# Hybrid encoder block on one core: hidden blocks 19 and 20 by seven products, and 22 sums of w_down quarters made by DRAM transfers

## The chip, the core and the metric

The kernel runs on one core of a Trainium2 chip. The metric is the device time in microseconds of one execution. Matmuls run on PE (TensorE), elementwise work on DVE (VectorE) and ACT (ScalarE); POOL (GpSimd) does a few small operations and issues some DMAs; SP issues nearly all others. All operands are float32, and every product is made of three matmuls of float32r parts: with a = a_hi + a_lo and w = w_hi + w_lo it is w_hi a_hi + w_hi a_lo + w_lo a_hi. ACT makes the high parts by a cast, DVE the low parts by a subtraction.

## The reference

```python
# SEQ = 512, D_MODEL = 1024, FFN_HIDDEN = 2816 (22 blocks of 128), DEPTH = 1
for l in range(DEPTH):
    h = rms_norm(x, attn_norm[l])
    proj = h @ w_in[l]      # q, k, v, forget logits, pool input, conv x/B/C, gates
    y_a = forgetting_attention(...) @ w_proj_attn[l]      # 8 heads x 64
    y_b = multiscale_pool(u, pool_w[l], pool_scale[l]) @ w_proj_pool[l]
    y_c = short_gated_conv(cv, cb, cc, conv_w[l]) @ w_proj_conv[l]
    mixed = gates[..., 0, :] * y_a + gates[..., 1, :] * y_b + gates[..., 2, :] * y_c
    x = x + mixed @ w_out[l]
    h = rms_norm(x, ffn_norm[l])
    a, b = jnp.split(h @ w_gate_up[l], 2, axis=-1)
    x = x + (jax.nn.silu(a) * b) @ w_down[l]
return rms_norm(x, final_norm)
```

## The kernel before, in words

Each engine runs a program written out by hand; semaphores tie them together, and no scheduler moves anything. The stages, in the order of the table STAGES, are: norm; front; pair (four attention passes of two heads each); mix and rounds (branch gates and projections); out (the product with w_out); ffn_first, ffn_head, turns and ffn_last (the 22 hidden blocks); down (the product with w_down).

A hidden block needs 128 gate columns and 128 up columns of w_gate_up over 1024 rows. A plain block (`gate_up`) does it in 2 units of 8 products of a 128 x 128 weight tile and 512 tokens. A turn (v counts them) does it by Winograd's scheme on quarters: 4 rows of weight tiles by gate or up, 256 tokens by half, seven products F11, F21, F2, F1, F3, F22, F4 of 4 tiles each. The sums of activations it needs (sums_hi, sums_lo) are made once; the sums of weight quarters are made in each turn by DVE (`turn_sums`, `turn_last_sum`), which also adds the partial products up (`turn_post`) and makes the hidden rows (`turn_hidden`). Blocks 0 to 3 are plain, 4 to 18 are the 15 turns, 19 to 21 are plain in ffn_last.

Two hidden blocks make a tile of down. `hid_sum(r)` makes tile r's four sums, `hidden_hi` and `hid_low` their parts. The product with w_down is by Winograd too, over R = 11 tiles: the first phase takes A11 with the quarter (2r, 1) and S1 with the sum of both quarters of block 2r, the later ones take sums with more quarters and the rest. Before the change DVE makes all sums of w_down: `first_sum` (11), two in each `second_sums` (22) and `third_sum` (11). `chain(r)` is the place of the running sum; for r of 3 and more it lies in the area that holds the operand of the plain blocks and turns.

Weights come by SP's queue into three slots of `raw` (load 6 of down into a spare place), their parts go to three slots of whi and wlo, in down to a ring of nine half slots. x2, the residual, is kept in DRAM (x2_kept) during the turns and comes back in ffn_last, one of four loads behind each unit from the third on.

POOL issues for each attention pass four small transfers of two rows of forget sums (L880, L882), those of passes 1 to 3 when the score products of the pass before are done (full6). Behind those of the last pass it waits for norm_var, which comes in ffn_first. PE waits for them (f_in) ahead of the score products.

Of the kernel before, what the change touches and what calls it, by code (L numbers as in the profile page):

```python
# [26 lines left out]
P = 128  # L27
# [9 lines left out]
          ("ffn_first", 1, 2), ("ffn_head", 1, 6), ("turns", 1, 105),  # L37
          ("ffn_last", 1, 6), ("down", 1, 77)]
# [7 lines left out]
TURNS = range(4, 19)  # L46
# [9 lines left out]
    "free2": dict(front=1, pair=1, mix=1, out=4, ffn_head=1, ffn_last=1),  # L56
    "free3": dict(front=1, pair=5, mix=1, out=4, ffn_head=1, ffn_last=1),
    "free4": dict(front=2, pair=4, mix=2, out=2, ffn_head=1, ffn_last=1),
    "free5": dict(front=3, pair=4, mix=1, out=2, ffn_head=1, ffn_last=1),
# [20 lines left out]
    "vector_step": dict(norm=11, front=23, pair=5, mix=6, rounds=8, ffn_first=3, ffn_head=5, turns=7, ffn_last=4,  # L80
# [30 lines left out]
def loads_before(stage, i, j):  # L111

    first, per = stage_of(stage)
    if stage in LATER + LAST_STAGES:
        first -= PARTS - LOADS
    if stage in LAST_STAGES:
        first -= PER_TURN * len(TURNS) - TURN_LOADS
    return (first + j + i * per) // SLOTS + 1


def hybrid_block(nc, x, attn_norm, w_in, b_forget, b_gate, w_proj_attn, pool_w, pool_scale,
# [26 lines left out]
    with ExitStack() as ctx:  # L148
# [36 lines left out]
        w_sums = nc.dram_tensor("w_sums", [16 * P, D // 2], F32, kind="Internal").ap()  # L185
        x2_kept = nc.dram_tensor("x2_kept", [S, D], F32, kind="Internal").ap()
# [189 lines left out]
        SUMMED = list(TILES.values()) + [0, 1, 9, 10]  # L376
# [116 lines left out]

        def down_raw(k, half, n=1):
# [62 lines left out]
        out_summed, sums_kept = sem("out_summed"), sem("sums_kept")  # L557
        mix_summed, mix_hi, mix_lo = sem("mix_summed"), sem("mix_hi"), sem("mix_lo")
# [32 lines left out]
        def _(sp):  # L591
            def load(stage, i, j, halves, width=P):
# [7 lines left out]
                elif stage == "ffn_last" and j < SLOTS:  # L600
                    v, part, sums = ((-2, F22, 3), (-1, F21, 4), (-1, F22, 4))[j]
                    v += len(TURNS)
                    sp.wait_ge(w_lo, turn_part(v, part) + 1)
                    sp.wait_ge(turn_summed, 4 * v + sums)
# [6 lines left out]
                for src, at in halves:  # L611
# [4 lines left out]
                                 ).then_inc(landed[s], 16)  # L616

# [152 lines left out]
            for j in range(3):  # L770
                for n, c in enumerate(gate_up_columns(19 + j)):
# [2360 lines left out]
```

## Time and profile before

| | |
|---|---|
| median of 3 runs | 770.66 us (770.55 to 770.76) |
| the profiled execution's own time | 770.3 us |
| its span, first to last instruction | 768.5 us |
| PE busy | 759.5 us (99%) |
| DVE, ACT, POOL busy | 649.4, 420.7, 18.3 us |
| moved by DMA | 99.46 MB, mean 129 GB/s |

The span is the part that the trace covers; 1.8 us of the execution lie around it. Matmuls are pipelined and their durations overlap, so what one costs is read from start to start. An idle time of an engine counts only where PE ends up waiting for it.

### The profile page before, as it was taken

How to read it: one execution, taken by the hardware profiler on the slowest of the kernel's cores; microseconds unless marked ns; L12 is line 12 of the kernel's file. 1: busy time of each engine (PE TensorE's matmuls, PEld its weight loads, DVE VectorE, ACT ScalarE, POOL GpSimd, SP SyncE). 2: the span in 40 equal slices, each digit the busy share in tenths (PEclk: the TensorE clock that was granted, in tenths of full speed). 3: DMA queues.
4: the chain of work that ended last, by engine and by line, in shares of the span. 5: the costliest groups of instructions: out<-in, count | busy, mean ns of one | idle time of the engine just before them, and what ended most of it. 6: DMA issues, size and time to landing. Idle time of an engine off the chain costs nothing.

```text
span 768.5 us, 12215 instructions
## 1 busy us (share of the span) xinstructions
PE 759.5 (99%) x4451; PEld 675.3 (88%) x4451; DVE 649.4 (85%) x1041; ACT 420.7 (55%) x712; POOL 18.3 (2%) x41
## 2 busy tenths in 40 slices
PE   8999999999999999999999999999999999999997
PEld 7888888888889999999988888999999998888885
DVE  7788976767798969777787899899999985899997
ACT  6536556646544646555455745555555552655554
POOL 2001100100000000000000000000000000000001
PEclk9999999999999999999999999999999999999999
DMA  8963542324133443344376533333333364443423
GB/s 301 306 202 82 166 111 56 84 55 110 46 93 83 111 127 93 83 110 113 107 269 197 192 111 94 103 106 110 110 101 98 106 209 147 141 161 133 149 89 110
DMA packets 133311, 99.46 MB, mean 129 GB/s; under 512 B 5932, under 2 KB 114532, under 8 KB 133252
## 3 DMA queue, kind: packets, MB, share of 16 engines
q1 hardware_dynamic: 132596, 98.35, 42.4%
q8 instruction: 36, 0.59, 0.3%
q10 hardware_dynamic: 144, 0.26, 0.1%
q14 instruction: 23, 0.19, 0.1%
q0 software_dynamic: 512, 0.07, 0.1%
HBM read 90.21 MB, written 8.39 MB: 128 GB/s over the span
## 4 chain that ended last, share of the span: by engine, by line
PE 98%; DMA 0%; issue 0%; ACT 0%; DVE 0%; POOL 0%; POOLq 0%; DVEq 0%
PE bank L917 10%; PE bank L913 10%; PE bank L915 10%; PE bank L1350 7%; PE bank L1348 7%; PE bank L1346 7%; PE bank L1161 4%; PE bank L1400 4%; PE bank L1159 4%; PE bank L1401 4%; PE bank L1402 4%; PE bank L1157 4%; PE bank L1195 2%; PE bank L1196 2%; PE bank L1197 2%; PE bank L1258 2%
## 5 line engine op out<-in xcount | busy, mean ns | idle before, releaser
L913 PE MATMUL bank<-operands,whi 128*128 128x512 f32 x352 | 137.9, 392 | 0.0
L917 PE MATMUL bank<-operands,wlo 128*128 128x512 f32 x352 | 137.1, 390 | 0.0
L915 PE MATMUL bank<-operands,whi 128*128 128x512 f32 x352 | 137.0, 389 | 0.0
L2078 DVE TENSOR_TENSOR wlo<-raw,whi 128x1024 fp32r<-128x1024 f32 x61 | 74.2, 1223 | 16.8 <-ACT whi L1466 16.0
L1466 ACT CAST whi<-raw 128x1024 fp32r<-128x1024 f32 x61 | 64.1, 1050 | 26.4 <-PE bank L917 7.6
L917 PEld LDWEIGHTS bank<-operands,wlo 128*128 128x128 f32 x352 | 66.1, 188 | 13.9
L915 PEld LDWEIGHTS bank<-operands,whi 128*128 128x128 f32 x352 | 66.1, 188 | 13.3
L913 PEld LDWEIGHTS bank<-operands,whi 128*128 128x128 f32 x352 | 66.1, 188 | 13.3
L1346 PE MATMUL bank<-sums_hi,whi 128*128 128x256 f32 x240 | 67.9, 283 | 0.0
L1348 PE MATMUL bank<-sums_lo,whi 128*128 128x256 f32 x240 | 67.9, 283 | 0.0
L1350 PE MATMUL bank<-sums_hi,wlo 128*128 128x256 f32 x240 | 67.9, 283 | 0.0
L1348 PE MATMUL bank<-operands,whi 128*128 128x256 f32 x180 | 50.9, 283 | 0.0
L1350 PE MATMUL bank<-operands,wlo 128*128 128x256 f32 x180 | 50.9, 283 | 0.0
L1346 PE MATMUL bank<-operands,whi 128*128 128x256 f32 x180 | 50.9, 283 | 0.0
L1346 PEld LDWEIGHTS bank<-sums_hi,whi 128*128 128x128 f32 x240 | 46.1, 192 | 0.0
L1348 PEld LDWEIGHTS bank<-sums_lo,whi 128*128 128x128 f32 x240 | 46.1, 192 | 0.0
L1350 PEld LDWEIGHTS bank<-sums_hi,wlo 128*128 128x128 f32 x240 | 46.1, 192 | 0.0
L1161 PE MATMUL bank<-sums_hi,wlo 128*128 128x256 f32 x160 | 45.3, 283 | 0.0
L1159 PE MATMUL bank<-sums_lo,whi 128*128 128x256 f32 x160 | 45.3, 283 | 0.0
L1157 PE MATMUL bank<-sums_hi,whi 128*128 128x256 f32 x160 | 45.2, 283 | 0.0
L2421 DVE TENSOR_TENSOR wlo<-raw,whi 128x1024 fp32r<-128x1024 f32 (+1 forms) x40 | 38.1, 952 | 3.2 <-ACT whi L1652 3.2
L2823 DVE TENSOR_TENSOR wlo<-raw,whi 128x1024 fp32r<-128x1024 f32 x30 | 36.6, 1220 | 4.1 <-ACT whi L1893 4.1
(323 smaller groups left out, 1995.9 us busy)
## 6 DMA issues: line engine op xcount, KB each, us to landing
raw<-in_w_in_dram SPq DMA_DIRECT2D x105, 256.0 KB, 3.3
raw<-in_w_gate_up_dram SPq DMA_DIRECT2D x88, 256.0 KB, 3.3
raw<-in_w_down_dram SPq DMA_DIRECT2D x53, 256.0 KB, 3.0
big_x<-in_x_dram SPq DMA_DIRECT2D x8, 512.0 KB, 5.3
tiles<-in_w_out_dram SPq DMA_DIRECT2D x4, 1024.0 KB, 7.2
w_sums<-tiles SPq DMA_DIRECT2D x4, 1024.0 KB, 7.2
raw<-w_sums SPq DMA_DIRECT2D x16, 256.0 KB, 3.1
raw<-in_w_out_dram SPq DMA_DIRECT2D x12, 256.0 KB, 3.5
```

Source lines behind the costliest of these rows:

```text
L913: nc.tensor.matmul(banks[b][:, 0:width], whi[:, s, w], op(hi + k * S), start=a, stop=False)
L915: nc.tensor.matmul(banks[b][:, 0:width], whi[:, s, w], op(lo + k * S), start=False, stop=False)
L917: mm = nc.tensor.matmul(banks[b][:, 0:width], wlo[:, s, w], op(hi + k * S), start=False, stop=z)
L1157: nc.tensor.matmul(to, wh[:, w], xh, start=first and k == 0, stop=False, skip_group_check=not first)
L1159: nc.tensor.matmul(to, wh[:, w], xl, start=False, stop=False, skip_group_check=not first)
L1161: mm = nc.tensor.matmul(to, wl[:, w], xh, start=False, stop=k == 3, skip_group_check=not first)
L1346: nc.tensor.matmul(to, wh[:, w], xh, start=first and k == 0, stop=False, skip_group_check=not first)
L1348: nc.tensor.matmul(to, wh[:, w], xl, start=False, stop=False, skip_group_check=not first)
L1350: mm = nc.tensor.matmul(to, wl[:, w], xh, start=False, stop=k == 3, skip_group_check=not first)
L1466: nc.scalar.copy(whi[:, s, :], raw[:, s, :]).then_inc(w_hi, 1)
L2078: nc.vector.tensor_tensor(wlo[:, s, :], raw[:, s, :], whi[:, s, :].bitcast(F32), ALU.subtract).then_inc(w_lo, 1)
L2421: nc.vector.tensor_tensor(part_at(wlo, r, j, n), src, part_at(whi, r, j, n).bitcast(F32), ALU.subtract).then_inc(w_lo, n)
```

## The change

Two things at once:

- TURNS grows from blocks 4..18 to 4..20, so blocks 19 and 20 go by seven products and ffn_last keeps block 21 alone, in banks 0 and 1. Since its two units fall into other slots, its loads take the raw slot of `last_slot(j)`, and the places of down's ring are moved by a slot. In the last turn DVE makes the hidden sums of tiles 0 and 1.
- 22 of the sums of w_down quarters are made in DRAM, in a new tensor down_sums of 2 x 1408 rows of 512: `copy_down(kind)` copies a quarter of each of the 11 block pairs, `add_down(kind)` adds a second by an accumulating DMA. POOL issues the first copy behind its transfers for the third attention pass, and the first add, the second copy and the second add behind those for the fourth. SP waits for both adds (down_added) before w_down's loads; in the first two phases of down one of a load's two transfers is now such a sum, in the first phase straight to `chain(r)`. `first_sum` is gone, and `second_sums` has one addition for two. Down's loads 3 and up now stand behind the wait for the end of block 21 on PE (used >= NU), where before only load 6 and up did. x2's four loads move to behind down's loads 6 to 9.

```diff
-          ("ffn_first", 1, 2), ("ffn_head", 1, 6), ("turns", 1, 105),
-          ("ffn_last", 1, 6), ("down", 1, 77)]
+          ("ffn_first", 1, 2), ("ffn_head", 1, 6), ("turns", 1, 119),
+          ("ffn_last", 1, 2), ("down", 1, 77)]
...
-TURNS = range(4, 19)
+TURNS = range(4, 21)
...
+def last_slot(j):
+
+    return (stage_of("turns")[0] - PARTS + LOADS + TURN_LOADS + j) % SLOTS
...
+        down_sums = nc.dram_tensor("down_sums", [2 * FH // 2, D // 2], F32, kind="Internal").ap()
...
+            at = (at + NU % SLOTS * 2 * S) % (2 * SLOTS * S)
...
@@ SP
-            for j in range(3):
-                for n, c in enumerate(gate_up_columns(19 + j)):
-                    load("ffn_last", 0, 2 * j + n, c)
-                    t = 2 * j + n - 2
-                    if t == 0:
-                        sp.wait_ge(used, turn_part(len(TURNS) - 1, F22) + 1)
-                    if t >= 0:
-                        sp.dma_start(big_x[:, t * D:(t + 1) * D], x2_kept[t * P:(t + 1) * P, :]
-                                     ).then_inc(x2_back, 16)
+            for n, c in enumerate(gate_up_columns(TURNS[-1] + 1)):
+                load("ffn_last", 0, n, c)
...
+            sp.wait_ge(down_added, 32)
             for r in range(R):
-                if r == SPARE:
+                if r == SLOTS:
                     sp.wait_ge(used, NU)
-                elif r == SPARE + SLOTS:
+                if r == 0:
+                    sp.wait_ge(used, turn_part(LAST_TURN, F22) + 1)
+                if r == SPARE + SLOTS:
                     sp.wait_ge(w_lo, NU + 2 * (SPARE - SLOTS) + 2)
-                else:
+                elif r < SLOTS - LAST_UNITS:
+                    turn_raw_read(LAST_UNITS + r)
+                elif r != SPARE:
                     sp.wait_ge(w_lo, NU - SLOTS + r + 1 if r < SLOTS else NU + 2 * (r - SLOTS) + 2)
                 sp.sem_inc(loads_begun, 1)
-                load_down(r, [(2 * r, 1), (2 * r, 0)])
+                load_down(r, [(down_block(2 * r, 1), down_raw(r, 0)),
+                              (down_sum(0)[r * P:(r + 1) * P, :], chain(r))])
+                if SPARE <= r < SPARE + TB:
+                    t = r - SPARE
+                    sp.dma_start(big_x[:, t * D:(t + 1) * D], x2_kept[t * P:(t + 1) * P, :]
+                                 ).then_inc(x2_back, 16)
...
-                load_down(R + r, [(2 * r, 0), (2 * r + 1, 0)])
+                load_down(R + r, [(down_sum(1)[r * P:(r + 1) * P, :], down_raw(R + r, 0)),
+                                  (down_block(2 * r + 1, 0), down_raw(R + r, 1))])
...
@@ POOL
+            down = w_down.rearrange("(r e p) c -> p r e c", e=2, p=P)
+            def summed_rows(kind):
+                return down_sum(kind).rearrange("(r p) c -> p r c", p=P)
+            def copy_down(kind):
+                c = 1 - kind
+                pool.dma_start(summed_rows(kind), down[:, :, 0, c * HALF:(c + 1) * HALF]
+                               ).then_inc(down_copied, 16)
+            def add_down(kind):
+                pool.wait_ge(down_copied, 16 * (kind + 1))
+                pool.dma_start(summed_rows(kind), down[:, :, kind, 0:HALF], accum_op=ALU.add
+                               ).then_inc(down_added, 16)
...
                     pool.dma_start(op(K2[a], S, slice(at, at + 2)).bitcast(F32), f_pair
                                    ).then_inc(f_in, 16)
+                if i == 2:
+                    copy_down(0)
+                elif i == 3:
+                    add_down(0)
+                    copy_down(1)
+                    add_down(1)
...
@@ PE
+            pe.wait_ge(turn_gates, 2 * LAST_TURN)
+            pe.wait_ge(turn_posted, 4 * LAST_TURN)
             gate_up("ffn_last", 0, 0)
             pe.wait_ge(turn_gates, 2 * len(TURNS))
             pe.wait_ge(turn_posted, 4 * len(TURNS))
-            for j in range(1, 3):
-                gate_up("ffn_last", 0, j)
...
@@ DVE
-            def first_sum(r):
-                dve.wait_ge(*landed_down(r))
-                if r == 3:
-                    dve.wait_ge(used, NU)
-                nc.vector.tensor_tensor(chain(r), down_raw(r, 0), down_raw(r, 1),
-                                        ALU.add).then_inc(summed, 1)
...
-                b12, b22 = raw[:, s, 0:HALF], raw[:, s, HALF:2 * HALF]
-                nc.vector.tensor_tensor(b12, b12, b22, ALU.add).then_inc(summed, 1)
+                b22 = raw[:, s, HALF:2 * HALF]
                 nc.vector.tensor_tensor(chain(r), chain(r), b22, ALU.add).then_inc(summed, 1)
```

The order on DVE at the end of the last turn before the change, and into the first plain block (bank6, bank5: partial products of the turn; wlo<-raw: low parts of a plain unit; tiles: hidden sums):

```order
L2831 TENSOR_TENSOR work<-bank6,work 128x256
L2078 TENSOR_TENSOR wlo<-raw,whi 128x1024
L2831 TENSOR_TENSOR work<-bank5,work 128x256
L2723 TENSOR_TENSOR operands<-tiles_32_50,operands 128x512
L2839 SCALAR_TENSOR_TENSOR tiles_32_50<-work 128x512
L2078 TENSOR_TENSOR wlo<-raw,whi 128x1024
L2709 TENSOR_TENSOR tiles_32_50<-tiles_32_50 128x512
```

The same place after the change, down to the first part of w_down (L2712):

```order
L2867 TENSOR_TENSOR work<-bank6,work 128x256
L2121 TENSOR_TENSOR wlo<-raw,whi 128x1024
L2745 TENSOR_TENSOR tiles_32_50<-tiles_32_50 128x512
L2750 SCALAR_TENSOR_TENSOR tiles_32_50<-tiles_32_50 128x256
L2753 SCALAR_TENSOR_TENSOR tiles_32_50<-tiles_32_50 128x256
L2745 TENSOR_TENSOR tiles_32_50<-tiles_32_50 128x512
L2750 SCALAR_TENSOR_TENSOR tiles_32_50<-tiles_32_50 128x256
L2753 SCALAR_TENSOR_TENSOR tiles_32_50<-tiles_32_50 128x256
L2867 TENSOR_TENSOR work<-bank5,work 128x256
L2759 TENSOR_TENSOR operands<-tiles_32_50,operands 128x512
L2875 SCALAR_TENSOR_TENSOR last_tile_32_52<-work 128x512
```

The hidden sums of tiles 0 and 1 stood behind the turn's last addition (work<-bank5) and a third unit's split, and now stand ahead of that addition.

On POOL, the end of its transfers of forget rows before the change:

```order
L880 DMA operands<-big_y 2x512
L882 DMA operands<-big_y 2x512
L880 DMA operands<-big_y 2x512
L882 DMA operands<-big_y 2x512
L887 TENSOR_TENSOR stat<-stat 128x4
```

And after it, from the last transfer for the third pass on:

```order
L925 DMA operands<-big_y 2x512
L906 DMA down_sums<-in_w_down_dram 128x11x512
L923 DMA operands<-big_y 2x512
L925 DMA operands<-big_y 2x512
L923 DMA operands<-big_y 2x512
L925 DMA operands<-big_y 2x512
L912 DMA down_sums<-in_w_down_dram 128x11x512
L906 DMA down_sums<-in_w_down_dram 128x11x512
L912 DMA down_sums<-in_w_down_dram 128x11x512
L936 TENSOR_TENSOR stat<-stat 128x4
```

The fourth pass's forget rows now stand behind the first copy, the rest of the DRAM transfers behind them.

On SP, from the last gate and up columns on, before the change:

```order
L777 DMA big_x<-x_kept 128x1024
L615 DMA raw<-in_w_gate_up_dram 128x4x128 x2
L777 DMA big_x<-x_kept 128x1024
L785 DMA raw<-in_w_down_dram 128x512 x12
L785 DMA early_49<-in_w_down_dram 128x512 x2
```

And after it, from load 5 of down on:

```order
L800 DMA raw<-in_w_down_dram 128x512
L800 DMA early_49<-down_sums 128x512
L800 DMA early_49<-in_w_down_dram 128x512
L800 DMA early_49<-down_sums 128x512
L819 DMA big_x<-x_kept 128x1024
L800 DMA raw<-in_w_down_dram 128x512
L800 DMA early_49<-down_sums 128x512
L819 DMA big_x<-x_kept 128x1024
```

x2's loads (big_x<-x_kept) stood among the plain blocks' loads and now stand among those of down.

## Rows read from the trace of the kernel before

**Rows 1.** The page, first part: span, and PE's busy time.

```profile
span 768.5 us, 12215 instructions
...
PE 759.5 (99%) x4451; PEld 675.3 (88%) x4451; DVE 649.4 (85%) x1041; ACT 420.7 (55%) x712; POOL 18.3 (2%) x41
```

**Rows 2.** The page, fourth part: the chain that ended last.

```profile
PE 98%; DMA 0%; issue 0%; ACT 0%; DVE 0%; POOL 0%; POOLq 0%; DVEq 0%
```

**Rows 3.** Windows (turns; plain blocks; down): PE, PEld, DVE, ACT, POOL busy, PEclk, DMA share, GB/s.

```profile
474.04:625.23 151.19, 151.19 (x1261) 151.19 (x1260) 139.89 (x220) 84.06 (x141) 0.00 (x0) 1.00 0.37 106
...
625.23:657.90 32.67, 32.67 (x147) 27.03 (x145) 21.00 (x31) 11.35 (x17) 0.00 (x0) 1.00 0.56 182
657.90:687.00 29.10, 29.10 (x130) 24.11 (x129) 28.00 (x43) 19.60 (x29) 0.00 (x0) 1.00 0.52 174
```

**Rows 4.** Timeline of PE at the borders (start us, us, engine, line, operation).

```profile
474.04 0.28 PE L1346 MATMUL bank<-operands,whi 128*128 128x256 f32 x1
...
625.23 0.40 PE L913 MATMUL bank<-operands,whi 128*128 128x512 f32 x1
```

**Rows 5.** Timeline of DVE, last turn and plain block 19.

```profile
625.12 1.23 DVE L2078 TENSOR_TENSOR wlo<-raw,whi 128x1024 fp32r<-128x1024 f32 x1 [1.32 <-ACT whi L1466]
628.94 0.69 DVE L2709 TENSOR_TENSOR tiles<-tiles 128x512 f32<-128x512 f32 x1
...
630.46 0.68 DVE L2709 TENSOR_TENSOR tiles<-tiles 128x512 f32<-128x512 f32 x1
```

**Rows 6.** Timeline of ACT, then of DVE, start of down.

```profile
661.30 1.28 ACT L1979 ACT_TABLE_LOAD   x1
...
662.60 0.68 DVE L2676 TENSOR_TENSOR early<-raw 128x512 f32<-128x512 f32 x1
663.24 0.69 DVE L2668 TENSOR_TENSOR operands<-raw,operands 128x512 fp32r<-128x512 f32 x1
...
664.45 0.69 DVE L2668 TENSOR_TENSOR operands<-early,operands 128x512 fp32r<-128x512 f32 x1
```

**Rows 7.** Timeline of POOL's DMA issues, third pass's last, fourth pass's first and last.

```profile
116.38 0.57 POOL L882 DMA_DIRECT2D operands<-big_y  x1
149.48 0.54 POOL L880 DMA_DIRECT2D operands<-big_y  x1 [32.52 <-PE bank L1089]
...
151.08 0.58 POOL L882 DMA_DIRECT2D operands<-big_y  x1
```

**Rows 8.** The page, third part (packets, MB, share) and sixth (KB, us to landing).

```profile
q0 software_dynamic: 512, 0.07, 0.1%
...
raw<-in_w_in_dram SPq DMA_DIRECT2D x105, 256.0 KB, 3.3
...
raw<-in_w_down_dram SPq DMA_DIRECT2D x53, 256.0 KB, 3.0
...
w_sums<-tiles SPq DMA_DIRECT2D x4, 1024.0 KB, 7.2
...
operands<-big_y POOLq DMA_DIRECT2D x16, 4.0 KB, 1.6
```

**Rows 9.** Windows of two stretches dense with transfers.

```profile
85.00:97.00 12.00, 12.00 (x69) 10.23 (x68) 10.88 (x20) 5.96 (x15) 0.00 (x0) 1.00 0.84 264
384.00:397.00 13.00, 13.00 (x66) 11.05 (x65) 9.67 (x15) 7.07 (x9) 0.00 (x0) 1.00 0.82 292
```

**Rows 10.** Timelines of SP, PE, ACT and DVE, fourth attention pass.

```profile
174.14 1.01 SPq L615 DMA_DIRECT2D raw<-in_w_in_dram  x2
...
180.39 0.28 PE L1087 MATMUL bank<-operands 128*128 128x256 f32 x1
...
186.23 1.06 ACT L1466 CAST whi<-raw 128x1024 fp32r<-128x1024 f32 x1
...
189.72 1.27 DVE L2307 TENSOR_SCALAR big_y<-big_y,stat 128x128 f32<-128x128 f32 x4
...
195.08 0.49 PE L1102 MATMUL bank<-ident,big_y 128*128 128x128 f32 x3
```

More of the change, by code:

```diff
@@ L55 @@
     "free1": dict(front=1, pair=2, mix=1, out=3, ffn_first=1, ffn_head=1, ffn_last=1),
[L56 to L59, printed above, removed]
+    "free2": dict(front=1, pair=1, mix=1, out=4, ffn_head=1),
+    "free3": dict(front=1, pair=5, mix=1, out=4, ffn_head=1),
+    "free4": dict(front=2, pair=4, mix=2, out=2, ffn_head=1),
+    "free5": dict(front=3, pair=4, mix=1, out=2, ffn_head=1),
     "free6": dict(front=2, pair=4, mix=1, out=2, ffn_first=1),
@@ L78 @@
     "v_lo_part": dict(pair=2),
-    "vector_step": dict(norm=11, front=23, pair=5, mix=6, rounds=8, ffn_first=3, ffn_head=5, turns=7, ffn_last=4,
+    "vector_step": dict(norm=11, front=23, pair=5, mix=6, rounds=8, ffn_first=3, ffn_head=5, turns=10, ffn_last=1,
                         down=3),
@@ L599, in load @@
                     sp.sem_inc(loads_begun, 1)
[L600 to L604, printed above, removed]
+                elif stage == "ffn_last":
+                    s = last_slot(j)
+                    turn_raw_read(j)
                     sp.sem_inc(loads_begun, 1)
@@ L616, in load, with turn_raw_read @@
                                  ).then_inc(landed[s], 16)
+            def turn_raw_read(m):
+                v, part, sums = ((-2, F22, 3), (-1, F21, 4), (-1, F22, 3))[m]
+                v += len(TURNS)
+                sp.wait_ge(w_lo, turn_part(v, part) + 1)
+                sp.wait_ge(turn_summed, 4 * v + sums)
             def columns(w, col):
@@ L781, in load_down, with down_block @@
-            def load_down(k, blocks):
+            for n, c in enumerate(gate_up_columns(TURNS[-1] + 1)):
+                load("ffn_last", 0, n, c)
+            def down_block(row, c):
+                return w_down[row * P:(row + 1) * P, c * HALF:(c + 1) * HALF]
+            def load_down(k, parts):
                 signal = spare_in if k == SPARE else landed[k % SLOTS]
-                for at, (row, c) in enumerate(blocks):
-                    sp.dma_start(down_raw(k, at),
-                                 w_down[row * P:(row + 1) * P, c * HALF:(c + 1) * HALF]
-                                 ).then_inc(signal, 16)
+                for src, to in parts:
+                    sp.dma_start(to, src).then_inc(signal, 16)
@@ L1311, in gate_up @@
             def gate_up(stage, i, j):
-                a = (2 * j + 2) % 6
+                a = (2 * j + 2) % 6 if stage == "ffn_head" else 0
                 k = j // 3 + 1
@@ L2009, in _ @@
             for rows in ROWS4:
-                act.wait_ge(summed, 3 * R + rows[-1] + 1)
+                act.wait_ge(summed, R + rows[-1] + 1)
                 for at, n in in_one(U_4 + rows[0], len(rows)):
@@ L2872, in _ @@
                 turn_post(v, 3, 3, 2, u, 1)
-                if last:
+                if not last:
+                    turn_lo(v + 1, F2, turn_sum(0, 2), 2)
+                else:
                     split_lo("ffn_last", 0, 1)
-                else:
-                    turn_lo(v + 1, F2, turn_sum(0, 2), 2)
+                    hid_sum(0)
+                    wait_free(dve, 1, "ffn_head", 0, 1)
+                    hid_sum(1)
                 dve.wait_ge(used, turn_part(v, F22) + 1)
```

78 lines of the change are left out of this document (32 added, 46 removed).

## The prediction

> **What bounds the kernel now.** The first view is the page: the engines' busy shares and the chain that ended last. PE, the matmul engine, is busy for 759.5 of 768.5 us [rows 1], and 98% of the chain is PE following PE [rows 2]. So time leaves only with matmuls that leave, and comes only with a wait that makes PE stand. The second view is the windows around the two stages that change [rows 3]: from 474.04 to 657.90 PE is busy for every us, DVE for 139.89 of 151.19 us in the turns and for 21.00 of 32.67 in the three plain blocks behind them. The third is PE's timeline at the borders [rows 4], by which the windows are cut; the durations there (0.28, 0.40) overlap, so what a matmul costs is its window divided by the count.
>
> **PE's work.** The 15 turns (seven products) run from 474.04 to 625.23: 151.19/15 = 10.08 us each. The three plain blocks run from 625.23 to 657.90: 32.67/3 = 10.89 us each [rows 3, 4]. A turn is 7 x 4 x 3 = 84 matmuls of 256 columns, a plain block 2 x 8 x 3 = 48 of 512, so columns fall by an eighth, but the narrow ones cost more per column: 10.08/84 = 0.120 us against 10.89/48 = 0.227, and 10.08 is 0.926 of 10.89. Blocks 19 and 20 become turns: 2 x (10.89 - 10.08) = 1.62 us less. Nothing else on PE changes in number: down keeps its products. Turns would end at 474.04 + 17 x 10.08 = 645.4, block 21 at 656.3, where down begins, for 657.9 before. Matmuls run at the same clock on both sides of the border (granted 1.00 in both windows, the 2.4 GHz level), so the pitches carry over.
>
> **The last turn and block 21.** I move the rows of the last turn [rows 5] by 2 x 10.08 = 20.16 us. DVE's second split for block 21 starts at 645.3 and takes 1.2 us. Behind it stand the hidden sums of tiles 0 and 1, ahead of the turn's last addition from its bank: 1.5 us each (628.94 to 630.46), so they end near 649.5. The turn's last addition, tile 9's low part, the turn's product, two more low parts and the first two w_down parts follow: seven of at most 0.6 us (the pitch of 512 columns in [rows 6]), to 653.7. PE wants all of it at 656.3: 2.6 us left. This backlog had three plain blocks to drain in and now has one; that is the cover which thins.
>
> **Start of down.** Load 3 and those behind it now wait on SP for PE to finish block 21, because a sum lands straight in the operand area; before, only the DVE sum waited. Issued at 656.5 and 656.9, at 3.0 us each [rows 8], they land near 660. ACT meanwhile does load 2's parts (two casts, 1.1), the last tile's high part behind scaled and hid_sum on DVE (659.8) and the table load (1.3 us [rows 6]), so it takes load 3 at 661.1, and DVE ends its low parts at 662.9. PE asks at 656.3 + 3 steps of 12 matmuls at 32.67/144 = 0.227 us, 664.4: 1.5 us left. Before, the same parts ended at 665.1 [rows 6] for a PE that asked at 657.9 + 8.2 = 666.1, so 1.0 was left. I charge nothing.
>
> **What leaves DVE.** Of the 44 quarter sums of w_down on DVE 22 go: 22 x 0.6 us of pitch (662.60 to 663.24 [rows 6]) = 13 us of DVE in down. That hurries only what PE already finds ready: between 657.90 and 687.00 PE is busy for 29.10 of 29.10 us with DVE at 28.00 [rows 3]. I credit nothing.
>
> **x2 comes back later.** Its four loads of 512 KB move from the plain blocks (182 GB/s in that window, rows 3) into down's loads 6 to 9. From 656.5 to load 10 there are 8 x 0.524 + 4 x 0.524 = 6.3 MB. Load 10 must be in 1.9 us ahead of PE (656.3 + 10 x 2.72 = 683.5), and data flows some 1.8 us behind the first issue: 23.3 us, or 270 GB/s. The two dense stretches of the trace moved 264 at a share of 0.84 and 292 at 0.82 [rows 9], so full engines give 314 to 356. It fits, by 3 us at 314.
>
> **The transfers.** One moves 11 x 128 rows of 2 KB, 2.88 MB. POOL issues the first copy behind the third pass's rows (116.9), and add, copy, add behind the fourth's (151.7) [rows 7]. The trace has no DRAM-to-DRAM and no adding transfer. For a copy the low end is 2.88 MB / 356 GB/s = 8 us, the high end the store of w_sums, 7.2 us for 1.05 MB [rows 8], so 20 us. An add also reads its target, twice a copy: 16 to 40. The three behind 151.7 take 40 to 100 us and end between 192 and 252. I take 16 for an add, since w_sums' row is a landing time with loads queued beside it, and so an end near 195. SP wants them near 644: never late.
>
> What they can cost is the loads beside them. The tightest of the fourth pass is issued at 174.14 and lands near 178 (issue 0.4 us apart, 3.3 [rows 8]); ACT takes it at 186.23, ahead of the second head's exponentials, and their probabilities end at 191.0 for a PE that asks at 195.08 [rows 10]. Allowance: 8.2 + 4.1 = 12.3 us. A pair of loads is 64 packets of 512 bytes an engine. If engines took one 2 KB packet of the transfers for each, at 2 KB / (314/16 GB/s) = 104 ns it would be 6.7 us later, at twice that for an add 13.3; fair halves by bytes, 1.7. Two of the three fit. I charge nothing. The Trainium skill's "DMA: Bandwidth & Descriptors", section "Queues, rings and completion order", says that an engine changes queues at packets that hold some 9 to 17 descriptors; by that a pair of loads would be interrupted 4 to 7 times, not 64, and the sum would stay at nothing. No row here shows it.
>
> POOL has to write the rows' descriptors itself, and the fourth pass's F rows stand behind the first copy. PE asks for them at 180.39 [rows 10]; they take 2.2 us to issue and 1.6 to land. So the copy may hold POOL until 176.6: 59.7 us, 42 ns a row. Below, it costs nothing. The nearest rows are those F issues, two rows in 0.54 us [rows 7], where the fixed part is not told apart: 270 ns a row if all of it were per row, near nothing if none. By packets it is 17 ns, for the 16 issues made 512 packets [rows 8], 32 each; I take that, 24 us for 1408 rows. The Trainium skill, "SBUF — State Buffer", "Who interferes with whom", speaks against the change here: descriptors that GpSimd writes wait while VectorE holds the port pair that the two share. The F issues, beside a DVE at work, all took 0.54 to 0.58, so the trace shows no such wait; by the rule POOL would take longer, and the sum would change only past 42 ns a row.
>
> **Sum.** Profiled: span 768.5 - 1.62 = 766.9, and 770.3 with the 1.8 around it becomes 768.7. The median of the runs, 770.66, lies 0.36 above the profiled run, so 769.0. That is 0.21% down, and 0.2% (1.54 us, to 769.12) is about what a measurement tells from no change: the forecast sits on that line.
>
> **Rivals.**
> 1. The transfers hold up the loads (slower). For: the allowance ends at 12.3/64 = 192 ns a packet, and twice 104 is over it; in the rounds from 232.8 on, a transfer still running would meet loads that are taken as they land. Against: fair sharing costs 1.7, and only 88 packets an engine exist per transfer. Price: 1.0 us at 208 ns, and at the high end (7.2 us per 32 packets = 225, doubled 450) 64 x 0.45 - 12.3 = 16.5. I take 5: 774.0. It decides from some 240 ns on.
> 2. Down starts late. For: 1.5 us at load 3, 2.6 at load 0, and x2 on the same queue. Price: at 250 GB/s 6.3 MB take 25.2 us, 1.9 late: 770.9, within 0.2%. Against: measured rates.
> 3. POOL is held past 176.6. At 270 ns a row the copy holds it 380 us, to 497; PE would stand from 180.4 to some 501: 320 us, 1089.
> 4. The saving isn't all there (a turn at the end pays a wait on DVE's backlog, where DVE is 93% busy): 0.8 of 1.62, 769.8.
>
> **Chances.** Forecast 0.66, rival 1 0.14, rival 2 0.11, rival 3 0.03, rival 4 0.06. The forecast's own range is 768.8 to 769.3 (0.1 of the runs' spread, 0.2 of small gaps); some 0.7 of it lies under 769.12. Faster: 0.66 x 0.7 and a little that DVE's relief might give: 0.48. Slower: 0.14 + 0.03 = 0.17. Within: 0.35. Range: down to 768.7; up to 771.1, which takes in rivals 2 and 4 and leaves out most of 1 and 3.
>
> **What would show it.** Right: PE's windows again without a gap, 17 turns at 10.08 us, down beginning 1.6 us earlier, POOL's copy issue under 60 us, the adding transfers landed before 232.8, landing times of w_in loads from 117 to 200 under 12 us. Wrong: idle time on PE at the score products (L1087) or probability transposes (L1102) of passes three and four, or on the first products of down behind w_down parts; or POOL issue rows of tens of us.

## The result and the profile after

The changed kernel takes 774.54 us (median of 4 runs, 772.36 to 775.52), the kernel before 770.71 in the same comparison: the ratio is 1.0046, with a 95% interval from 1.0025 to 1.0067. It is slower, and above the range of the forecast (768.7 to 771.1). The profiled execution took 772.36 us.

The first and third part of the page and its list of DMA issues answer to [rows 1, 8]: PE is busy for as long as before in a span 2.0 us longer, although it has fewer columns to do.

```profile
span 770.5 us, 12395 instructions
...
PE 759.6 (99%) x4523; PEld 677.9 (88%) x4523; DVE 648.2 (84%) x1039; ACT 426.1 (55%) x724; POOL 24.5 (3%) x45
...
q0 software_dynamic: 4800, 11.60, 6.4%
...
down_sums<-in_w_down_dram POOLq DMA_DIRECT2D x4, 2816.0 KB, 21.2
```

The windows over turns, block 21 and down, cut as in [rows 3], show the saving that was forecast: 171.35/17 = 10.08 us a turn, 10.91 for block 21, and no idle time on PE. The turns began at 477.71 and not at 474.04, so 3.67 us were lost ahead of them. Of these 0.37 were there before the first transfer (a load that the kernel before issues at 112.03 is issued at 112.40); the fourth attention pass makes the other 3.3.

```profile
477.71:649.06 171.35, 171.35 (x1430) 171.35 (x1428) 158.88 (x250) 95.31 (x160) 0.00 (x0) 1.00 0.36 103
649.06:659.97 10.91, 10.91 (x51) 9.02 (x49) 10.77 (x18) 5.76 (x10) 0.00 (x0) 1.00 0.41 142
659.97:690.00 30.03, 30.03 (x134) 24.89 (x133) 24.04 (x37) 19.68 (x30) 0.00 (x0) 1.00 0.82 280
...
659.97:764.92 104.95, 104.95 (x469) 86.97 (x467) 90.96 (x128) 61.25 (x94) 2.14 (x3) 1.00 0.46 159
```

The chain of waits around the only long gap (start, us, what; the fourth attention pass) says where. The second half of a weight load, issued at 166.05, lands 16.49 us later; ACT casts it, DVE makes its low parts, and only then does DVE take the first head's row maxima (L2335), which free the banks for the second head's score products (L1136). Before, the same load landed 3.5 us behind its issue at 165.66, at 169.1, and ACT took it at 179.02.

```profile
166.05 16.49 DMA raw<-in_w_in_dram
182.54 0.02 issue
182.56 1.05 ACT whi L1516
...
183.64 1.23 DVE wlo L2121
...
184.90 0.29 DVE big_y L2335
...
185.25 0.38 PE bank L1136
```

The window around it in the kernel before has 24 matmuls and no idle time; the changed kernel's, shown under the run again, has 9 and 2.3 us without any. The rest of the 3.3 us is matmuls that start far apart behind the gap.

```profile
182.50:187.00 4.50, 4.50 (x24) 3.72 (x23) 3.78 (x17) 3.54 (x10) 0.00 (x0) 1.00 0.40 116
```

The timeline of ACT and DVE in the kernel before shows the same three steps without a wait: parts at 180.10, row maxima at 181.36.

```profile
179.02 1.05 ACT L1466 CAST whi<-raw 128x1024 fp32r<-128x1024 f32 x1
180.10 1.23 DVE L2078 TENSOR_TENSOR wlo<-raw,whi 128x1024 fp32r<-128x1024 f32 x1 [0.97 <-ACT whi L1466]
181.36 0.29 DVE L2291 CUSTOM_DVE_ANT_0 big_y<-bank,flat 128x128 f32<-128x128 f32 x1
```

POOL's timeline of its issues (start, us) answers to [rows 7]: one copy in the third pass, add and copy back to back in the fourth, and the second add once the copy has landed.

```profile
117.33 1.14 POOL L906 DMA_DIRECT2D down_sums<-in_w_down_dram  x1
...
152.04 2.04 POOL L912 DMA_DIRECT2D down_sums<-in_w_down_dram  x1
153.20 1.96 POOL L906 DMA_DIRECT2D down_sums<-in_w_down_dram  x1
182.46 1.87 POOL L912 DMA_DIRECT2D down_sums<-in_w_down_dram  x1 [27.30 <-DMA down_sums<-in_w_down_dram]
```

How a load comes to 16 us is in the DMA queues of two stretches, 160 to 171 us beside the first add and 174 to 180 beside the second copy (packets, MB, share of 16 engines; q0 carries the transfers, q1 the loads).

```profile
q0 software_dynamic: 910, 1.86, 91.0%
q1 hardware_dynamic: 908, 0.46, 21.0%
```

```profile
q0 software_dynamic: 492, 2.01, 86.8%
q1 hardware_dynamic: 504, 0.25, 14.7%
```

The two queues moved as many packets as each other. One of an add took 0.910 x 16 x 11 us / 910 = 176 ns and one of a copy 169, one of a load 41 and 28. The 64 packets an engine of a load are thus stretched to 64 x 217 ns = 13.9 us beside an add. The load issued at 154.7 needed until 172.4; the one issued at 165.6 stood behind it in SP's queue and then met the second copy.

### The profile page after: what moved, and what is told of

It reads as the page before. It is cut to its first block, busy times and chain, and to the rows that moved or that the text cites. A ratio compares the mean times of both kernels' runs of the same rounds, so it can differ in the third digit from the quotient of the medians.

```text
span 770.5 us, 12395 instructions
## 1 busy us (share of the span) xinstructions
PE 759.6 (99%) x4523; PEld 677.9 (88%) x4523; DVE 648.2 (84%) x1039; ACT 426.1 (55%) x724; POOL 24.5 (3%) x45
## 4 chain that ended last, share of the span: by engine, by line
PE 95%; DMA 3%; DVE 1%; issue 1%; ACT 1%; POOL 0%; POOLq 0%; SPq 0%; DVEq 0%
PE bank L962 9%; PE bank L966 9%; PE bank L964 9%; PE bank L1399 7%; PE bank L1397 7%; PE bank L1395 7%; PE bank L1451 4%; PE bank L1210 4%; PE bank L1208 4%; PE bank L1449 4%; PE bank L1206 4%; PE bank L1450 4%; PE bank L1244 2%; PE bank L1245 2%; PE bank L1246 2%; DMA raw<-in_w_in_dram 2%
## 5 line engine op out<-in xcount | busy, mean ns | idle before, releaser
L962 PE MATMUL bank<-operands,whi 128*128 128x512 f32 x320 | 125.4, 392 | 0.0
L966 PE MATMUL bank<-operands,wlo 128*128 128x512 f32 x320 | 124.7, 390 | 0.0
L964 PE MATMUL bank<-operands,whi 128*128 128x512 f32 x320 | 124.6, 389 | 0.0
L1397 PE MATMUL bank<-sums_lo,whi 128*128 128x256 f32 x272 | 77.0, 283 | 0.0
L1395 PE MATMUL bank<-sums_hi,whi 128*128 128x256 f32 x272 | 77.0, 283 | 0.0
L1399 PE MATMUL bank<-sums_hi,wlo 128*128 128x256 f32 x272 | 77.0, 283 | 0.0
L1516 ACT CAST whi<-raw 128x1024 fp32r<-128x1024 f32 x57 | 59.9, 1050 | 29.8 <-PE bank L966 7.6
L964 PEld LDWEIGHTS bank<-operands,whi 128*128 128x128 f32 x320 | 60.1, 188 | 12.1
L962 PEld LDWEIGHTS bank<-operands,whi 128*128 128x128 f32 x320 | 60.1, 188 | 12.1
L1397 PE MATMUL bank<-operands,whi 128*128 128x256 f32 x204 | 57.7, 283 | 0.0
L1399 PE MATMUL bank<-operands,wlo 128*128 128x256 f32 x204 | 57.7, 283 | 0.0
L1395 PE MATMUL bank<-operands,whi 128*128 128x256 f32 x204 | 57.7, 283 | 0.0
L1397 PEld LDWEIGHTS bank<-sums_lo,whi 128*128 128x128 f32 x272 | 52.2, 192 | 0.0
L1210 PE MATMUL bank<-sums_hi,wlo 128*128 128x256 f32 x160 | 45.3, 283 | 0.0
L1208 PE MATMUL bank<-sums_lo,whi 128*128 128x256 f32 x160 | 45.3, 283 | 0.0
L1206 PE MATMUL bank<-sums_hi,whi 128*128 128x256 f32 x160 | 45.2, 283 | 0.0
L1944 ACT CAST whi<-raw 128x1024 fp32r<-128x1024 f32 x34 | 35.6, 1046 | 11.5 <-PE bank L1399 9.3
## 6 DMA issues: line engine op xcount, KB each, us to landing
down_sums<-in_w_down_dram POOLq DMA_DIRECT2D x4, 2816.0 KB, 21.2
```

The lines of the kernel that those rows point to most:

```text
L962: nc.tensor.matmul(banks[b][:, 0:width], whi[:, s, w], op(hi + k * S), start=a, stop=False)
L964: nc.tensor.matmul(banks[b][:, 0:width], whi[:, s, w], op(lo + k * S), start=False, stop=False)
L966: mm = nc.tensor.matmul(banks[b][:, 0:width], wlo[:, s, w], op(hi + k * S), start=False, stop=z)
L1206: nc.tensor.matmul(to, wh[:, w], xh, start=first and k == 0, stop=False, skip_group_check=not first)
L1208: nc.tensor.matmul(to, wh[:, w], xl, start=False, stop=False, skip_group_check=not first)
L1210: mm = nc.tensor.matmul(to, wl[:, w], xh, start=False, stop=k == 3, skip_group_check=not first)
```

## The experiments

Twelve runs, one of them the changed kernel again; times are medians, ratios are taken against runs of the kernel before on the same chip.

| kernel | us | ratio, 95% interval |
|---|---|---|
| again (changed kernel once more) | 773.91 | 1.0041 [1.0027, 1.0054] |
| no_sums | 769.19 | 0.9976 [0.9967, 0.9985] |
| copies_only | 769.25 | 0.9979 [0.9970, 0.9988] |
| dve_order | 769.36 | 0.9980 [0.9972, 0.9989] |
| before_plus | 775.10 | 1.0054 [1.0041, 1.0066] |
| two_two | 768.96 | 0.9977 [0.9968, 0.9986] |
| turns_only | 771.61 | 1.0011 [1.0002, 1.0020] |
| small | 772.70 | 1.0028 [1.0017, 1.0038] |
| order_before | 771.01 | 0.9998 [0.9989, 1.0006] |
| sums_only | 770.93 | 0.9998 [0.9989, 1.0007] |
| both | 769.31 | 0.9973 [0.9963, 0.9984] |
| in_rounds | 774.87 | 1.0045 [1.0032, 1.0058] |

### again

> The changed kernel once more, nothing edited, for a second profile and the spread of its runs. Theory T (the transfers delay loads of the attention passes, and one of them makes PE stand before the second head's score products of the fourth pass): a gap of 2 to 6 us at 182.5 to 187 in the profile, and the median again 3 to 4 us above before, 774 to 775. The profiled run so far was at 772.4 while three others were at 774.5 to 775.5; if T is the whole story, a profile of a longer run shows a longer stall at the same place (4.5 to 5.5 us), or a second stall by another delayed load. Rival L (late start of down, or x2's loads): the additional 2 to 3 us stand on PE between 650 and 690.

Measured 773.91 us (773.86 to 774.42), the profiled run 773.86 with a span of 772.0: 1.5 longer than the first profile, of which 0.3 were there before the first transfer (POOL issued it at 117.65, not 117.33). The windows of the stall and of the 3 us behind it, first of the changed kernel's first profile, then of this one (PE busy and count, ..., granted clock, DMA share, GB/s):

```profile
182.50:187.00 4.50, 2.18 (x9) 1.19 (x9) 3.19 (x11) 1.08 (x2) 1.83 (x1) 1.00 0.98 211
187.00:190.00 3.00, 3.00 (x15) 2.45 (x14) 2.42 (x13) 2.98 (x10) 0.00 (x0) 1.00 1.11 202
```

```profile
182.50:187.00 4.50, 2.15 (x10) 1.42 (x8) 2.92 (x9) 1.05 (x1) 1.87 (x1) 0.92 1.01 220
187.00:190.00 3.00, 3.00 (x9) 2.37 (x8) 2.37 (x14) 2.60 (x9) 0.00 (x0) 0.55 1.10 194
```

The stand of PE is the same (2.3 us idle), but here the clock granted behind it is the 1.2 GHz level for 3.4 us (186.3 to 189.7), and PE gets 9 matmuls done in 3 us where it had done 15. That is the missing 1.2 us; the expectation that a longer run has a longer stall was wrong. The runs without a profile at 774.5 to 775.5 had a mean granted clock of 0.997 against 0.998 for the one at 772.36, as this kernel's had 0.996 and 0.997; that they carry the same second price is argued from that, not shown. What decides whether the clock falls stays open, for the two stands were equally long.

### no_sums

```diff
-            sp.wait_ge(down_added, 32)
...
-                              (down_sum(0)[r * P:(r + 1) * P, :], chain(r))])
+                              (down_block(2 * r, 0), chain(r))])
...
-                if i == 2:
-                    copy_down(0)
-                elif i == 3:
-                    add_down(0)
-                    copy_down(1)
-                    add_down(1)
```

> The changed kernel without the four DRAM transfers and without SP's wait for them; where a load took a sum it takes the block (2r, 0) of w_down, which has the same size. It leaves out the 22 sums of w_down quarters, so the output is not the block's. T: nothing else of the change costs time, so 769.0 (768.7 to 769.4), no gap at 182 to 187. Rival L (the late start of down, the last turn's backlog, or loads straight into the operand area cost something): 770.5 or more. Rival S (only the stall seen in the profile, 3.3 us, comes from the transfers, and the 2 to 3 us by which other runs are longer has another cause): 771 to 772.

Measured 769.19 us, by theory T. All that the change loses hangs on the four transfers, and without them the kernel stands where the forecast put it (769.0). Rivals L and S fall.

### copies_only

```diff
-            sp.wait_ge(down_added, 32)
+            sp.wait_ge(down_copied, 32)
...
                 elif i == 3:
-                    add_down(0)
                     copy_down(1)
-                    add_down(1)
```

> The changed kernel with the two copies (behind the rows of the third and of the fourth pass) and without the adding transfers; SP waits for the copies, and the loads take blocks (2r, 0) in the sums' place, so the 22 sums are left out. T with packet sharing as the mechanism: one copy of 2.88 MB lasts 12 to 13 us and delays the loads beside it by some 9 us, as the first copy did; the one in the fourth pass, issued at 152, is through at 165, before the load issued at 165.2 is served, which so lands on time: no stall, 769.0 to 769.5. Rival: any transfer in the fourth pass costs (it begins too near to the loads): 771 or more.

Measured 769.25 us, no gap. The copy in the fourth pass was issued at 152.03 and landed at 164.74, ahead of the critical load. A transfer there is not harmful in itself. Whether one that still runs at 165 does harm is another question: in two_two below an add ran until 172.8 without a gap on PE.

### dve_order

```diff
-                split_lo("pair", i, 4)
-
                 for a in range(2):
                     lg = big_y
...
                                             ).then_inc(row_max, 1)
+                split_lo("pair", i, 4)
                 for a in range(2):
                     dve.wait_ge(exp_done
```

> The changed kernel with all four transfers; only DVE's low parts of the pass's last projection unit are moved behind the row maxima of both heads. T: the load issued at 165.2 lands as late as in the changed kernel (182.5), but DVE no longer makes the row maxima wait for it, so the 3.3 us gap at 182.5 to 186.7 goes and the median falls by 3 to 5 us, to 769 to 771. Rival A (ACT's high parts, in order ahead of the exponentials, are the real hold): the gap stays at 2 us or more. Rival B (the next delayed load, landing at 202.7, then decides): some 1 to 3 us at 200 to 206 stand in place of it.

Measured 769.36 us. The timeline of ACT and DVE: ACT still waits 3.71 us for the load, but the row maxima started at 181.25 and the low parts come last, at 185.22.

```profile
181.25 0.29 DVE L2334 CUSTOM_DVE_ANT_0 big_y<-bank,flat 128x128 f32<-128x128 f32 x1 [1.68 <-PE bank L1138]
...
183.12 1.05 ACT L1516 CAST whi<-raw 128x1024 fp32r<-128x1024 f32 x1 [3.71 <-DMA raw<-in_w_in_dram]
...
185.22 1.22 DVE L2121 TENSOR_TENSOR wlo<-raw,whi 128x1024 fp32r<-128x1024 f32 x1
```

So a load 13 us late costs nothing here but through that one place in DVE's order. Rival A falls, and B too: the window behind has no idle time.

```profile
182.50:187.00 4.50, 4.50 (x23) 3.85 (x23) 4.19 (x16) 3.85 (x11) 1.87 (x1) 1.00 0.94 210
187.00:190.00 3.00, 3.00 (x15) 2.45 (x15) 2.12 (x4) 3.00 (x9) 0.00 (x0) 1.00 1.09 187
```

### before_plus

```diff
 (the kernel before)
+                if i == 2:
+                    copy_down(0)
+                elif i == 3:
+                    add_down(0)
+                    copy_down(1)
+                    add_down(1)
...
+                if r == 0:
+                    sp.wait_ge(down_added, 32)
```

> The kernel before, with the four DRAM transfers added at the places of the change and SP's wait for them ahead of w_down's loads; their result is not used and everything else stays as before. Theory T (the transfers delay the load issued at 165 us, DVE's low parts of it stand ahead of the row maxima, PE stands 3.3 us and then runs some 3 us at the 1.2 GHz level, 1 to 1.5 us more): before plus 3.3 to 5, so 774.3 to 776. Rival (the delay needs something else of the change, or the extra wait on SP costs): under 772, or a gap elsewhere than at 182 to 187.

Measured 775.10 us: 4.45 us by the medians for the transfers and SP's wait alone. The waits on ACT, DVE and PE from 175 to 192 us (engine and line waited for what: us in total, times, longest) are those of the changed kernel, and the clock behind the stand is low here too:

```profile
DVE wlo L2106 <- ACT whi L1494: 4.5, 1, 4.5
ACT whi L1494 <- DMA raw<-in_w_in_dram: 3.6, 1, 3.6
...
PE bank L1115 <- DVE stat L2319: 2.7, 1, 2.7
```

```profile
182.50:187.00 4.50, 1.77 (x8) 1.34 (x7) 2.78 (x8) 1.04 (x1) 1.87 (x1) 0.81 0.82 177
187.00:190.00 3.00, 3.00 (x12) 2.44 (x11) 2.40 (x13) 2.46 (x9) 0.00 (x0) 0.72 1.13 203
```

### two_two

```diff
                 if i == 2:
                     copy_down(0)
+                    copy_down(1)
                 elif i == 3:
                     add_down(0)
-                    copy_down(1)
+                    pool.wait_ge(full[6], count("full6", "pair", 3, 2))
                     add_down(1)
```

> The changed kernel with both copies behind the third pass's rows, the first add behind the fourth's and the second add only behind the fourth pass's own second score products (some 184 us). T, with the second copy queued behind the first add as what makes the load issued at 165.2 so late: alone beside an add that ends by 173 it lands at 170 to 176, before 179 when it is wanted, so no gap: 769.0 to 770. Rival Q (any transfer beside the load delays it by 64 packets of some 0.2 us, 13 us, so 178 to 179): up to 1 us of the gap stays, 769.5 to 771. Rival P (two copies in a row in the third pass now delay that pass's load, landed and wanted 8 us apart with one copy): a new gap of 2 to 5 us at 145 to 150.

Measured 768.96 us. The load issued at 154.93 landed 17.4 us later, at 172.4, as in the changed kernel. The next (165.4) stood behind it but then, the add having landed at 172.8, had the engines to itself, and its halves landed 8.0 and 8.5 us after their issues (3.1 and 3.5 in the kernel before), at 174.3, with 4.9 us to spare. The windows:

```profile
182.50:187.00 4.50, 4.50 (x23) 3.72 (x22) 3.78 (x19) 3.37 (x10) 1.87 (x1) 1.00 0.42 118
187.00:190.00 3.00, 3.00 (x15) 2.49 (x14) 1.92 (x5) 2.65 (x9) 0.00 (x0) 1.00 1.02 152
```

This tells the delay's two parts apart: of the 13 us in the changed kernel 5 are those of a load behind a delayed load, and the other 8 come from the transfer that it meets itself. Rivals Q (up to 1 us of the gap left, 769.5 to 771) and P (a stall in the third pass) did not come, though P was near: the third pass's load landed 0.94 us ahead of ACT.

### turns_only

```diff
-                              (down_sum(0)[r * P:(r + 1) * P, :], chain(r))])
+                              (down_block(2 * r, 0), down_raw(r, 1))])
...
+            first_sum(0)
             down_lo(0)
+            first_sum(1)
             down_lo(1)
             second_lo(0)
+            first_sum(2)
...
+                nc.vector.tensor_tensor(b12, b12, b22, ALU.add).then_inc(summed, 1)
```

> One part of the change alone: blocks 19 and 20 by seven products, but no DRAM transfers; DVE makes the 22 sums of w_down quarters as before, the first three of them among the low parts at the start of down. If DVE's 13 us in down are hidden, as the prediction had it: 769.2, as without transfers at all. But the first sums now stand in the short stretch between the last turn and down, 3 x 0.6 = 1.8 us against 1.5 left at load 3: 0.3 to 1 us of waits on PE at 660 to 668 is what I expect, 769.2 to 770.2. Rival R (the relief of DVE is what makes the two blocks possible): 771 or more, the gaps at 657 to 670.

Measured 771.61 us, beyond what I expected: 2.4 more than without any sums at all. The windows of 40 us from some 3 us into down, of no_sums and of this kernel (PE, PEld, DVE busy, ...), show DVE nearly full and PE standing for 1.2 us, all of it at 686 to 693, not in the short stretch that I had named:

```profile
659.90:700.00 40.10, 40.10 (x178) 33.20 (x178) 34.30 (x48) 27.74 (x41) 0.00 (x0) 1.00 0.68 238
```

```profile
659.80:700.00 40.20, 39.02 (x169) 31.05 (x168) 38.10 (x58) 24.80 (x36) 0.00 (x0) 1.00 0.58 203
...
700.00:740.00 40.00, 40.00 (x179) 33.10 (x178) 39.21 (x54) 23.30 (x33) 0.00 (x0) 1.00 0.45 158
```

The standing is about half of the loss. From down's first matmul to its last PE takes 104.7 us in no_sums (657.00 to 761.68) and 106.9 in this kernel (656.35 to 763.28), 2.2 more, which is nearly the 2.4 of the medians. So the two more turns don't pay without the relief of DVE.

### small

```diff
-        down_sums = nc.dram_tensor("down_sums", [2 * FH // 2, D // 2], F32, kind="Internal").ap()
+        down_sums = nc.dram_tensor("down_sums", [4 * 2 * FH // 2, P], F32, kind="Internal").ap()
...
+                for b in range(4):
+                    pool.dma_start(summed_rows(kind)[:, :, b, :],
+                                   down[:, :, kind, b * P:(b + 1) * P], accum_op=ALU.add
+                                   ).then_inc(down_added, 16)
```

> The changed kernel with each transfer in four parts of 128 columns each, and the sums kept in DRAM in four blocks of 128 columns, so that each of its rows is 512 bytes, as those of the loads, and not 2 KB. Theory Q (an engine takes one packet of a queue for one of another, so a load's 64 packets wait for 64 large ones): packets are a quarter of the size, the load issued at 165.2 is late by some 64 x 0.05 to 0.08 = 3 to 5 us only, within its slack of 9.9, and the gap at 182.5 is gone: 769 to 770; the transfers take longer. Rival W (the loads wait for the bytes or for the engines' memory access, whatever the packets): the load is as late as before and the gap stays: 772 to 775.

Measured 772.70 us. Q's mechanism held where it could be tested. From 170 to 175 us the queues moved

```profile
q0 software_dynamic: 978, 0.49, 79.5%
q1 hardware_dynamic: 978, 0.49, 49.7%
```

one for one again, now at 0.795 x 16 x 5 us / 978 = 65 ns for a packet of an add. The load issued at 165.84 landed at 176.25, 6.5 us late (its second half took 10.0 us, 3.5 before) where I had said 3 to 5, and the gap at 182 was gone. But the time was not: the transfers lasted longer (the four adds until 180.7), the copies went in 4 KB packets all the same, and the next load met both. The chain:

```profile
175.15 15.89 DMA raw<-in_w_in_dram
...
191.06 1.06 ACT whi L1524
192.12 2.19 ACT big_y L1659 x8
...
194.55 2.65 DVE big_y L2359 x4
197.19 0.60 DVE operands L2137
...
197.93 1.85 PE bank L1159 x10
```

PE stood 2.1 us from 195.8 ahead of the probabilities' transposes, with the clock at the lower level for 3.4 us behind it. The stall had moved one load on, but not all of it is the load's: DVE's four multiplications L2359 took 2.65 us, where the same four took 1.27 in the kernel before (L2307, [rows 10]). They ran while POOL issued its second four adds (191.1 to 198.9). That is 1.4 us more in the chain, and what the late load would have cost without it is not shown.

### order_before, sums_only, both

The first is the move in DVE's order made in the kernel before; the second the DRAM sums, placed as in two_two and used by down, in the kernel before; the third two_two with dve_order's edit as well.

```diff
 (the kernel before, order_before)
-                split_lo("pair", i, 4)
...
+                split_lo("pair", i, 4)
                 for a in range(2):
                     dve.wait_ge(exp_done
```

```diff
 (the kernel before, sums_only)
-                load_down(r, [(2 * r, 1), (2 * r, 0)])
+                load_down(r, [(down_block(2 * r, 1), down_raw(r, 0)),
+                              (down_sums[r * P:(r + 1) * P, :], chain(r))])
...
-            first_sum(0)
```

> A control: the kernel before with nothing but the move of DVE's low parts of the pass's last projection unit behind the row maxima of both heads. In the kernel before that load lands 9.9 us ahead of ACT, so there is no wait that the move could take away: 770.7, the same within 0.1%. If instead it gains about 1.5 us, then what the kernel with that move alone gained over the changed one was not only the stall. If it loses 0.3 us or more, the parts come late for the projections behind.

> The other part of the change alone: blocks 19 to 21 plain as before, the 22 sums made by DRAM transfers (both copies in the third pass, the adds apart in the fourth, the placement that showed no stall) and loaded in the sums' place. DVE is relieved of 22 x 0.6 = 13 us in down, and PE was already without gaps there: if the relief alone is worth nothing, 770.7 (770.4 to 771.0), the same as before. Rival: DVE's relief hurries the end of the kernel (chain behind the last product), 769.5 or less.

> The changed kernel with both cures: the spread placement of the transfers and DVE's low parts behind the row maxima. Each alone already left no gap on PE in the fourth pass (768.96 and 769.36), so both together have nothing more to take away: 769.0 to 769.3, 0.2% under before. Under 768.7 would say that something of the stall was left in each.

Measured 771.01, 770.93 and 769.31 us, the first two as expected, the third at the upper edge. The move alone is worth nothing, so what dve_order won over the changed kernel was the stall. Thirteen microseconds less of DVE alone are worth nothing either (0.9998). The two cures together are no better than one.

### in_rounds

```diff
 (two_two)
-                    pool.wait_ge(full[6], count("full6", "pair", 3, 2))
+                    pool.wait_ge(used, weight_part(1, T1) + 1)
                     add_down(1)
```

> The spread placement, but the second add starts in the second of the projection rounds (some 250 us) and not in the fourth attention pass. There loads are taken 0 to 5 us after they land, the third of each round as it lands. By one load packet for each packet of the add (217 ns a pair), a load of 64 packets beside it is 10 to 13 us late, and at least two of them meet the add: I expect a stall on PE of 5 to 10 us and slowly clocked matmuls behind it, 774 to 781. Rival (the rounds have slack that the landing times don't show, in parts made ahead): under 771.

Measured 774.87 us, 5.9 more than two_two and at the lower edge of what I expected. The add ran from 257.9 to 278.4; the load issued at 265.9 landed 13.1 us behind its issue (3.4 in the kernel before). From 255 to 290 us the waits are

```profile
DVE flat L2449 <- DMA raw<-in_w_in_dram: 7.5, 1, 7.5
ACT whi L1703 <- DMA raw<-in_w_in_dram: 6.5, 1, 6.5
```

and PE stood three times, 1.7, 2.2 and 0.8 us. The granted clock stayed at 1.00 behind these: that part of the expectation was wrong.

## Why the prediction was wrong, step by step

- **PE's work.** Right to the hundredth: 10.08 us a turn, down with no idle time in its 104.95 us from the first matmul to the last, the same length as before. no_sums at 769.19 is the forecast's 769.0.
- **Last turn and start of down.** Right. The first two w_down parts were to be ready 2.6 us ahead of PE; they ended at 657.2 for a PE that asked at 659.97, so 2.8. Load 3's low parts were to have 1.5 us left; they ended at 666.7 for a PE that asked at 659.97 + 8.17 = 668.1, so 1.4.
- **What leaves DVE, credit nothing.** Right for the relief alone (sums_only), but the two parts are not separate terms: with the two more turns, DVE's relief is worth 771.61 - 769.19 = 2.4 us. I had it as a by-product, where it is what lets the 1.62 us be kept.
- **x2.** Right: no gap on PE from 659.97 to 690, with 280 GB/s moved.
- **Length of the transfers.** The first copy took 12.6 us (bound 8 to 20), an add 21.2 (bound 16 to 40, 16 taken); the last landed at 203.7, not 195. The second add began only at 182.46, since it waited 27.3 us for a copy that stood behind the first add.
- **POOL.** Wrong by far on the safe side: 1.1 to 2.0 us an issue for 1408 rows, not 24. The fourth pass's rows were never held up, and rival 3 had nothing to stand on. The Trainium skill, "SBUF — State Buffer", "Who interferes with whom", would have POOL's descriptors wait while VectorE holds the shared ports; no such wait shows in these issue rows. What does show is the other side, which I had not looked for: DVE's multiplications of the probabilities beside the first add's issue (152.04 to 154.08) took 1.85 us, where they take 1.27 in the kernel before (151.28). In the changed kernel nothing in the chain of the stall is of this kind; in small it is.

```profile
151.66 1.85 DVE L2351 TENSOR_SCALAR big_y<-big_y,stat 128x128 f32<-128x128 f32 x4
```

- **Loads beside the transfers: the step that failed.** I charged nothing, and it cost 3.3 us in the profile and 4.5 to 5.4 in the medians (before_plus over before; the changed kernel over no_sums). Three things were wrong in it. First, the load: I called the one at 174.14 the tightest, with 12.3 us. The one at 165.25 had 9.9, ACT's take at 179.02 less its landing; and nothing behind it, because DVE's low parts stand ahead of the row maxima in DVE's order, and those free PE's banks. I had looked for loads that are taken soon after they land, and not for what stands behind the take. Second, the price of a packet: one for one was among my cases, at 104 ns for a copy and 208 for an add, where the trace has some 169 and 176. The add's case came to 13.3 us, more than even the allowance of 12.3, and I set it aside as one case in three. From the 176 my estimate is 64 x (217 - 28) = 12.1 us of delay for a load beside an add; the one issued at 154.7 was 13.8 us late (17.6 us from its first issue to its last landing, 3.8 before). Third, the queue: a load's delay is passed on to the load behind it (5 us by two_two), which then meets the next transfer, 13 us in all. The two cases of mine that "fitted" did so under an allowance that was not the smallest.
- **The rule that I leaned on.** The records of both queues came in equal numbers (910 to 908), which agrees with the round-robin in the Trainium skill, "DMA: Bandwidth & Descriptors", "Queues, rings and completion order". What I drew from it was wrong: being interrupted seldom saves nothing when each turn of the other queue is as many packets long. By the rule rightly read, a load of 64 packets waits for 64 of the other's, however they are batched (the counts can't tell in what batches); at the measured 176 ns that is 11.3 us, and the longer packets of its own make it the 12.1.
- **Rivals.** Rival 1 came true in kind, at 14% and with its point of decision put at 240 ns a packet; 176 were enough. Its 774.0 was near the 774.5 by luck: the 5 us were picked between 1.0 and 16.5, and for another load. Rival 2 (down starts late) and rival 4 fall by no_sums.

## What to carry to other kernels

A bulk transfer beside tuned loads costs each load that it meets one of its packets for each of theirs, so price it as the load's packet count times the other's packet time, let the delay run on to the loads queued behind, and hold that against the slack of every load in the stretch, read up to the first engine that PE waits for. Issue such transfers apart from each other and where the next load is not wanted for 15 us; two_two did the same transfers as the changed kernel and is 0.23% faster than the kernel before instead of 0.5% slower. Look at DVE too while POOL issues them. And test a relief together with what it makes room for: here each of the two parts alone brought nothing or lost 0.1%, and the two together 0.2%.

## What the runs showed of the hardware

- A copy from DRAM to DRAM with rows of 2 KB moved as 4 KB packets of 159 ns (median), 12.6 to 13.0 us for 2.88 MB; an adding transfer of the same rows as 2 KB packets of 176 ns, 20.5 to 21.7 us. Cut into rows of 512 bytes, the add's packets took 65 ns, the copy's stayed at 4 KB.
- While both queues had packets waiting, they moved as many packets as each other, whatever the sizes: 910 of 2 KB to 908 of 512 bytes, 492 of 4 KB to 504, and 978 of 512 bytes to 978.
- A load's packet of 512 bytes took 41 ns beside an add and 28 beside a copy.
- DVE's TENSOR_SCALAR took longer beside POOL's issue of a large transfer: four of them 1.85 us in the changed kernel and 2.65 in small, where they took 1.27 in the kernel before. Its subtractions for the low parts did not (1.21 at 153.44, beside the same issues).
- After PE had stood for 2.1 to 2.7 us, its clock fell to the 1.2 GHz level for 3.4 us in three profiles (again, before_plus, small), and stayed at 2.4 GHz in two (the changed kernel's first, after 2.3 us; in_rounds, after 1.7 and 2.2). Such a stall can thus cost 1.2 us more (again against the first profile), and does so in some executions and not in others.
